# State inputs of two neighbouring tiles made together, the real parts first and then the imaginary ones, in alternating row groups

## What is computed

```
bu = einsum('blgc,gpc->blgp', u, b_bar)            # state inputs, complex
a  = broadcast(lam_bar)                            # one complex factor per state channel
h  = associative_scan(combine, (a, bu), axis=1)    # h_t = lam_bar * h_{t-1} + bu_t
h  = h + a_cum * h0
y  = real(einsum('blgp,gcp->blgc', h, c_mat)) + d_skip * u
y  = gelu(y);  y = y * sigmoid(y @ w_glu)
```

## Time and profile before

| what | value |
|---|---|
| runs | 1525.0, 1530.35, 1530.5 us, median 1530.35 |
| profiled execution | 1525.81 us, of which the span is 1523.6 us |
| TensorE busy | 1469.6 us (96%) |
| VectorE busy | 1265.6 us (83%) |
| ScalarE busy | 985.4 us (65%) |
| GpSimd busy | 144.4 us (9%) |
| mean granted TensorE clock | 0.974 of full speed |

### The profile page before, as it was taken

One profiled execution on the slowest core, in us unless ns is written; L12 is line 12 of the kernel. 1 busy time (PEld: TensorE's weight loads), 2 busy tenths in 40 slices (PEclk: granted clock), 3 DMA queues, 4 the chain that ended last, 5 costly groups with the idle time before them and its releaser, 6 DMA issues.

```text
span 1523.6 us, 22861 instructions
## 1 busy us (share of the span) xinstructions
PE 1469.6 (96%) x7443; PEld 1187.9 (78%) x7443; DVE 1265.6 (83%) x1669; ACT 985.4 (65%) x1295; POOL 144.4 (9%) x191
## 2 busy tenths in 40 slices
PE   6998899999998889999999999999999999999998
PEld 5664466999998568888888888888888888888886
DVE  8988994666644898889888889888888888988997
ACT  6111353544432677787787787778778778778774
POOL 2177700000000120000000000000000000001000
PEclk9998797999999999999999999999999999999999
DMA  6601253555464479999999999999999999999993
GB/s 238 237 28 56 62 179 134 174 166 169 141 179 160 158 285 387 371 365 371 379 352 380 366 371 375 370 364 371 372 371 357 379 376 359 372 380 362 383 394 125
DMA packets 217376, 434.84 MB, mean 285 GB/s; under 512 B 10673, under 2 KB 56909, under 8 KB 217052
## 3 DMA queue, kind: packets, MB, share of 16 engines
q1 hardware_dynamic: 212854, 416.99, 76.3%
q0 software_dynamic: 3840, 13.62, 2.4%
q10 hardware_dynamic: 622, 3.45, 0.6%
HBM read 423.47 MB, written 11.03 MB: 285 GB/s over the span
## 4 chain that ended last, share of the span: by engine, by line
PE 85%; DVE 4%; issue 1%; ACT 1%; DVEq 0%
PE bank L1451 21%; PE bank L1455 20%; PE bank L1456 20%; PE bank L1278 3%; PE bank L1282 3%; PE bank L1281 3%; PE bank L1476 2%; PE bank L1293 2%; PE bank L1297 1%; PE bank L1296 1%; PE bank L970 1%; PE bank L1229 1%; PE bank L1245 1%; PE bank L1113 1%; PE bank L1248 1%
## 5 line engine op out<-in xcount | busy, mean ns | idle before, releaser
L2356 DVE TENSOR_TENSOR split<-raw_w,split 128x1024 fp32r<-128x1024 f32 x672 | 783.6, 1219 | 50.1 <-ACT split L1822 48.9
L1822 ACT ACTIVATE split<-raw_w 128x1024 fp32r<-128x1024 f32 x672 | 688.9, 1061 | 105.1 <-PE bank L1451 103.9
L1451 PE MATMUL bank<-split,xgr 128*128 128x512 f32 x896 | 359.2, 401 | 6.1 <-DVE split L2356 6.0
L1455 PE MATMUL bank<-split,xgr 128*128 128x512 f32 x896 | 354.3, 395 | 0.0
L1456 PE MATMUL bank<-split,xgr 128*128 128x512 f32 x896 | 354.2, 395 | 0.0
L1451 PEld LDWEIGHTS bank<-split,xgr 128*128 128x128 f32 x896 | 169.0, 189 | 44.2 <-DVE split L2356 6.4
L1456 PEld LDWEIGHTS bank<-split,xgr 128*128 128x128 f32 x896 | 168.9, 188 | 40.2
L1455 PEld LDWEIGHTS bank<-split,xgr 128*128 128x128 f32 x896 | 169.1, 189 | 37.9
L1451 PE MATMUL bank<-split,hbr 128*128 128x512 f32 x448 | 178.7, 399 | 0.0
L1455 PE MATMUL bank<-split,hbr 128*128 128x512 f32 x448 | 176.9, 395 | 0.0
L1456 PE MATMUL bank<-split,hbr 128*128 128x512 f32 x448 | 176.8, 395 | 0.0
(11 more groups left out here) (450 smaller groups left out, 1844.2 us busy)
## 6 DMA issues: line engine op xcount, KB each, us to landing
raw_w<-in_moe_gate SPq DMA_DIRECT2D x112, 1024.0 KB, 7.2
raw_w<-in_moe_up SPq DMA_DIRECT2D x112, 1024.0 KB, 7.8
raw_w<-in_moe_down SPq DMA_DIRECT2D x112, 1024.0 KB, 7.1
ring<-in_w_gate SPq DMA_DIRECT2D x11, 1024.0 KB, 5.5
ring<-in_w_up SPq DMA_DIRECT2D x11, 1024.0 KB, 8.0
ring<-in_w_down SPq DMA_DIRECT2D x8, 1408.0 KB, 7.7
ring<-in_w_in SPq DMA_DIRECT2D x5, 2048.0 KB, 10.9
ring<-in_w_out SPq DMA_DIRECT2D x2, 2048.0 KB, 8.3
```

The costliest lines, as they stand in the source:

```text
L1451: first = mm(out, hi, place[:, s, 0, cols], start=start, stop=False)
L1455: mm(out, lo, place[:, s, 0, cols], start=False, stop=False)
L1822: A(place[:, s, 0, :], raw_w[:, at:at + BLOCK], ACT.Copy).then_inc(sem("high_ready"), 1)
L2356: TT(place[:, s, 1, :], raw_w[:, at:at + BLOCK], place[:, s, 0, :].bitcast(F32), ALU.subtract).then_inc(sem("low_ready"), 1)
```

## The change

The fill order takes the groups two at a time. Behind groups j and j+1 (j even) come four state inputs: real j, real j+1, imaginary j, imaginary j+1. TensorE makes all four when it comes to `("bur", j)` with j even; neighbours lie in different row groups of the array. ScalarE copies the sample columns in the new order, since it walks the list. VectorE does `state_tile(j)` and `state_tile(j+1)` behind each other, and its two waits on `raw_taken` count by the new order.

```diff
-    for j, group in enumerate(groups):
-        f += group + [("bur", j), ("bui", j)]
+    for j in range(0, NJ, 2):
+        f += groups[j] + groups[j + 1] + [("bur", j), ("bur", j + 1), ("bui", j), ("bui", j + 1)]
@@ state_inputs(j), TensorE
-                rows = slice(32 * (j % 4), 32 * (j % 4) + 32)
-                for r, name in enumerate((("bur", j), ("bui", j))):
-                    out = open_fill(name)
-                    mm(out[:, 0:T], b_m[rows, j // 4, r, :], uT[rows, j // 4, :],
-                       start=True, stop=True).then_inc(full(name), 1)
+                for r, kind in enumerate(("bur", "bui")):
+                    for i in (j, j + 1):
+                        rows = slice(32 * (i % 4), 32 * (i % 4) + 32)
+                        out = open_fill((kind, i))
+                        mm(out[:, 0:T], b_m[rows, i // 4, r, :], uT[rows, i // 4, :],
+                           start=True, stop=True).then_inc(full((kind, i)), 1)
@@ TensorE's walk
-                elif kind == "bur":
+                elif kind == "bur" and name[1] % 2 == 0:
                     state_inputs(name[1])
@@ state_tile(j), VectorE
-                dve.wait_ge(sem("raw_taken"), 2 * j + 1)
+                dve.wait_ge(sem("raw_taken"), 4 * (j // 2) + 1 + j % 2)
...
-                dve.wait_ge(sem("raw_taken"), 2 * j + 2)
+                dve.wait_ge(sem("raw_taken"), 4 * (j // 2) + 3 + j % 2)
```

## The result

| | before | after |
|---|---|---|
| median (runs) | 1529.62 us (4, 1525.0 to 1530.5) | 1540.26 us (4, 1538.31 to 1541.4) |
| profiled execution | 1525.81 us, span 1523.6 | 1541.4 us, span 1539.3 |
| mean granted clock | 0.974 | 0.965 |

The ratio is 1.0076, 95% interval 1.0062 to 1.009: slower by 0.6 to 0.9%, 1.3 us from the 1539 forecast. In the functions of TensorE and VectorE around the change the lines stand one further down now: L983 is the state input (L982 before), L992 the projection, L1013 the key, L1066 and L1090 half swap and spread, L1585 ScalarE's copy, L2037 and L2048 the first operation and the last scan of a state tile.

A forecast was written before the change was run, and what follows sets the result against it. The prediction took the state stage's chain through VectorE's last scan as the bound, with TensorE and VectorE feeding each other through seven banks. Held banks delay that scan 11.4 us, giving 1537.2 to 1541.7, stated as 1539, range 1532 to 1547.

The forecast's parts named there:

- Overlap: State inputs on TensorE: neighbours in different row groups overlap, a set of four takes 1.2 us instead of 2.4, saving 9.
- no overlap: Rival for the state input sets: they still take 2.4 us, so 13.8 us slower, 1539.6; chance 8%.
- Held banks: State stage: four banks wait for two tiles of VectorE, 7.8 us, leaving TensorE three; later fills wait too.
- walk: Step-by-step count of tile starts through the state stage: last scan at 170.0 instead of 158.6, 11.4 us later.
- some 7: Step at k3, ahead of tiles 10 and 11: of 10.9 us behind at tile 11's end, some 7 arise here.
- from a few us to over 10: Expected sign in the trace: growth of TensorE's waits for VectorE's last scan, at the key ahead of k0 and at k3.
- The clock: Projections q2, k0, k3 behind TensorE's waits: 5.73 us each assumed; at 1.2 GHz throughout the loss would be 18.4 us.
- full clock throughout: Case with q2, k0 and k3 at 4.04 us each: the last scan only 6.6 us later.
- The tail: From tile 11's end to the last scan: the same 24.8 us as before plus some 0.5 for ks 2 and ke 2.
- Faster: Rival in the state stage: five sets ahead of VectorE's waits save 1.2 us each, 6 us, 1519.8; chance 5%.
- About nothing: Rival in the state stage: clock stays up and VectorE's idle times are overestimated, +1 to +5 us, 1527 to 1531; chance 12%.
- The sum: End of the state stage: last scan 170.0 - 158.6 = 11.4 us later, giving 1537.2 or 1541.7, stated as 1539.

The follow-up runs named there:

- e1: Changed kernel, but TensorE makes both inputs of the first tile, then both of the second, same banks: 1539.45 us, 1.0074 of the kernel before.
- e2: Changed kernel with the set's four banks dealt out by tile (real j, imaginary j, real j+1, imaginary j+1): 1534.91 us, 1.0047 of the kernel before.
- e4: Changed kernel with all pairs, k0 and k3 moved ahead of the short fills of their double groups: 1530.78 us, 1.0021 of the kernel before.
- e7: Changed kernel with all pairs, only k3 moved ahead of the short fills of its double group: 1531.57 us, 1.0025 of the kernel before.
- e6: Changed kernel with only tiles 6/7, 8/9, 10/11 paired, k3 first in its group, k0 ahead of keys 2 and 3: 1525.31 us, 0.9985 of before.
- e5: Changed kernel with added matmuls, results unread, ahead of fills that wait for banks: 1533.07 us, 1.0031 of the kernel before.
- e3: Changed kernel with tiles 8 to 11 done singly as in the kernel before, other pairs kept: 1528.48 us, 1.0007 of the kernel before.
- e10: Kernel before with six matmuls, results unread, added ahead of the wiT transposes: 1525.82 us, 0.9991 of the kernel before.
- e9: e6 with six matmuls, results unread, added ahead of the wiT transposes: 1524.2 us, 0.9974 of the kernel before.

## Why the prediction was right

**Overlap: right, for a wider reason.** Sets take 1.21 us where I took 1.2. All 64 state input records together, in 50 to 175 us (busy us, mean ns), before and after:

```profile
L982 PE MATMUL bank<-ring,params 32*128 32x280 f32 x64 | 20.9, 442 | 4.4 <-DVE ring L2047 4.4
```

```profile
L983 PE MATMUL bank<-ring,params 32*128 32x280 f32 x64 | 12.9, 528 | 2.9 <-DVE ring L2048 2.9
```

8.0 us of TensorE saved instead of 9: two of the sets stand at half clock and take 2.24 (at 73.20 and at 148.35), and the eighth, mixed with L1090 from 162.04 on, takes 2.4. The rival "no overlap" falls with it. That the alternation makes the overlap was taken over from the change and is wrong (e1).

**Held banks: right, step by step.** The walk against the timeline:

| | walk | measured |
|---|---|---|
| idle ahead of tiles 2, 4, 6, 8, 10 | 1.1, 6.8, 1.4, 2.9, 9.9 | 1.42, 7.73, 2.21, 3.04, 10.70 |
| tile 2 starts | 76.1 | 74.72 |
| tile 4 starts | 90.7 | 90.39 |
| tile 6 starts | 107.0 | 107.54 |
| tile 8 starts | 117.7 | 118.31 |
| tile 10 starts | 136.9 | 138.34 |
| tile 11 ends | 144.7 | 146.07 |
| last scan ends | 170.0 | 172.04 |

The key, k3 and bur 2 wait for L2048, as counted from the list. e2, e4 and e7 show the mechanism by itself. The tiles began 1.4 to 1.9 us earlier than I walked (tile 0 at 65.33, not 67.2). The walk took the 8.8 us for VectorE's group 1 from the earlier trace rows; it took 6.7 here, 58.59 to 65.33. The difference is in three groups of operations (L2056, L2057 and L2087 before): 1.92, 1.77 and 1.82 us before, 1.33, 1.32 and 0.79 after. Before, GpSimd turned back tile 0 beside them; after, tile 0 isn't scanned yet and GpSimd has nothing to do. The DMA share is 1.0 in both at 58 to 64. e1 and e4, with group 1 first, have the short times too, and e6, with tile 0 first, the long ones; no run changes GpSimd's work alone. The first of the three with GpSimd's rows, before and after:

```profile
63.83 1.92 DVE L2056 TENSOR_TENSOR low<-low,ring 128x1120 f32<-128x1120 f32 x1
...
64.51 1.85 POOL L800 TENSOR_TENSOR ring<-ring 128x272 f32<-128x272 f32 x1
```

```profile
60.15 1.33 DVE L2057 TENSOR_TENSOR low<-low,ring 128x1120 f32<-128x1120 f32 x1
...
69.32 0.76 POOL L797 TENSOR_TENSOR ring<-ring 128x272 f32<-128x272 f32 x1 [34.75 <-DVE ring L2048]
```

From tile 9 to tile 11 the lateness grows from 5.0 to 12.4 us; the walk had "some 7" for this step. One sign was badly set: TensorE's waits for the last scan were to grow "from a few us to over 10", but before they came to 12.8 us already (4.4, 3.0, 2.9 and 2.5); after, they come to 23.2.

**The clock: right in place and direction, too small in size.** Taking 5.73 for q2, k0 and k3 left 0.6, 0.3 and 0.8 us out, and the set ahead of q2 another 1.0: 2.7 of TensorE, inside the range that I had named. This is the term that was sized too low. Between the rule of the Trainium skill (page "TensorE: Matmul & The Clock Gate", section "HAM oscillation — how this bites in real kernels") and my 5.73, the trace agrees with the rule for the three bursts that the walk turns on: each started cold, at 0.50 in the windows shown for k0 and k3. It doesn't for the two half swaps at 94.36, which took 0.71 us at 1.00 behind 2.22 us of waiting. The lower clock's price here is 2.0 to 2.5 us for each of the three, above my 1.7 and well under the 4.04 more of an all-cold projection. What the text underrated is the share: 4.8 of its 11.4 us (1.7, 1.4 and 1.7) hung on the clock, and e5 shows 7.9 of 13.5. Its case of the full clock throughout, 6.6 us, can be held against e5, where the last scan is 5.6 us late.

**The tail: 26.0 us instead of 25.3** (146.07 to 172.04).

**The other rivals.** "Faster" decided on whether TensorE would reach k3 and the key ahead of k0 after the tiles before them; it reached both first and waited 2.64 and 3.11 us. "About nothing" needed a milder clock than the profiled one and a stage that gives waits back. The second half of it exists, but at tiles 5 and 10 and not at ks and ke: e3 shows the old order giving back most of the lateness of tile 4. It could not help here because the step at tile 10 comes behind it.

**The sum:** 13.5 us by the last scan instead of 11.4. That the median, 1540.26, lies 1.3 us from 1539 is partly luck. In the walk, the 2.7 us that the clock took more and 0.7 of the tail stand against 1.9 that VectorE's group 1 took less; and 1539 itself was a point put between two levels of the kernel before. From 1528, about the middle of that kernel's medians, 1528 + 11.4 is near the forecast, 1528 + 13.5 - 0.7 = 1540.8 near the result.

## What to carry to other kernels

With banks dealt out in turn, fusing the producers of two consumers saves the producer's time and makes the banks stay taken until the second consumer is done. Before fusing, count which fill meets each held bank (here the one 7 places behind): a short fill whose reader is in no hurry may wait there, a long one that the next tile depends on may not, and moving it ahead of four short ones was worth 9.9 us. A wait of an engine with a variable clock costs its length and then the slower work behind it; keep the engine busy through it, or move the wait to where nothing long follows.

## What the runs showed of the hardware that I had not expected

- Two runs of four state input records in different row groups, one behind the other, take 1.22 us, nearly what the alternated ones take (1.21; e1), and as one run of four does alone (1.21). The work behind the set starts 1.15 us after the set in both orders. In e1 the second tile's real part started 0.01 us behind the first tile's and 0.56 us ahead of the first tile's imaginary part, which is issued before it: TensorE did not take matmuls of two row groups in the order of issue. What it does when one of them has to wait for its bank was not tried.
- VectorE's L2056 over 128x1120 took 1.92 us at 63.83 before, beside GpSimd's L800 over 128x272 with 1.85; after, the same operation took 1.33 at 60.15 with GpSimd idle, and L800 0.76 at 71.48 beside work of a state tile. It isn't always VectorE that is slower: at 148.94 after, its operation took 1.33 and GpSimd's beside it 1.84.
- Twelve to fourteen records of 128x64 weights over 224 columns (2.48 to 2.86 us) in the wait just ahead, and eight or ten in the wait before that for k0 and k3, brought q2, k0 and k3 from 6.1 to 6.5 us down to 4.01 to 4.04 (e5). They wrote partitions 64 to 127 of a bank in whose other half a live result stands.
- A projection at 5.73 us can stand where the trace shows no long pause ahead of it: k0 and k3 in e10 (0.96 us ahead of k0's set, none ahead of k3). What lowers the clock there stays open; e6 and e9, with another order and pairs, have the same two at 3.94 and 4.04.
